# One map instead of two: the difference of two softmax maps formed before the transpose, in a two-block transformer on one core

## The reference, cut to what matters

```python
logits = jnp.einsum('bqhmd,bkhmd->bhmqk', qb, k).astype(jnp.float32) * scale + bias
logits = jnp.where(rel >= 0, logits, -jnp.inf)
p = jax.nn.softmax(logits, axis=-1)
w = p[:, :, 0] - lam * p[:, :, 1]
return jnp.einsum('bhqk,bkhe->bqhe', w.astype(v.dtype), v)
```

## Time and profile before

| | us |
|---|---|
| median of 3 runs | 4071.55 (4066.73 to 4072.94) |
| span of the profiled execution, first to last instruction | 4059.8 |
| PE busy | 3739.4 (92%) |
| DVE busy | 2398.3 (59%) |
| ACT busy | 1795.8 (44%) |
| POOL busy | 301.1 (7%) |
| PE's share of the chain that ended last | 83% |

### The profile page before, as it was taken

One profiled execution on the slowest core, in us unless ns is written; L12 is line 12 of the kernel. 1 busy time (PEld: TensorE's weight loads), 2 busy tenths in 40 slices (PEclk: granted clock), 3 DMA queues, 4 the chain that ended last, 5 costly groups with the idle time before them and its releaser, 6 DMA issues.

```text
span 4059.8 us, 52830 instructions
## 1 busy us (share of the span) xinstructions
PE 3739.4 (92%) x19920; PEld 2885.1 (71%) x19920; DVE 2398.3 (59%) x3434; ACT 1795.8 (44%) x2906; POOL 301.1 (7%) x385
## 2 busy tenths in 40 slices
PE   8998897998999587998999998899999999889998
PEld 7885575666787355555887776788777878657877
DVE  7865945887875876986774327566333332564332
ACT  3336644897333754886322326422233222453222
POOL 0110001110210001000220000111000000000001
PEclk9999587999999677999999999999999999999999
DMA  7551013997653014995774320277323223302222
GB/s 274 180 164 53 2 63 123 348 369 258 212 189 113 1 54 147 369 364 201 269 269 158 107 91 8 103 235 234 109 87 125 97 90 104 146 22 89 95 95 75
DMA packets 165090, 618.38 MB, mean 152 GB/s; under 512 B 18668, under 2 KB 20245, under 8 KB 163709
## 3 DMA queue, kind: packets, MB, share of 16 engines
q1 hardware_dynamic: 118384, 433.15, 30.3%
q0 software_dynamic: 42240, 154.16, 11.8%
q10 hardware_dynamic: 4238, 27.90, 1.8%
HBM read 595.94 MB, written 16.31 MB: 151 GB/s over the span
## 4 chain that ended last, share of the span: by engine, by line
PE 83%; DVE 8%; ACT 4%; issue 2%; DMA 2%; SPq 0%; ACTq 0%; DVEq 0%; POOL 0%; POOLq 0%; PEldq 0%
PE psum L2243 23%; PE psum L2256 12%; PE psum L830 12%; PE psum L2011 8%; PE psum L915 5%; PE psum L2030 4%; PE psum L982 4%; PE psum L759 3%; PE psum L1199 1%; PE psum L1209 1%; PE psum L767 1%; DVE spare L1305 1%; DMA ring<-wtile 1%; PE psum L1967 1%; PE psum L1483 1%
## 5 line engine op out<-in xcount | busy, mean ns | idle before, releaser
L783 ACT CAST small_r<-ring 128x1024 fp32r<-128x1024 f32 x264 | 276.1, 1048 | 1075.1 <-PE psum L830 335.5
L787 DVE TENSOR_TENSOR ring_r<-ring,small_r 128x1024 fp32r<-128x1024 f32 x264 | 322.7, 1225 | 686.7 <-ACT small_r L783 686.2
L783 ACT CAST PB_r<-ring 128x1024 fp32r<-128x1024 f32 x344 | 357.5, 1050 | 567.8 <-PE psum L2243 326.8
L787 DVE TENSOR_TENSOR ring_r<-ring,PB_r 128x1024 fp32r<-128x1024 f32 x344 | 414.2, 1222 | 270.6 <-ACT PB_r L783 269.2
L2243 PE MATMUL psum<-H_r,ring_r 128*128 128x512 f32 x1344 | 335.2, 391 | 0.0
L2243 PE MATMUL psum<-H_r,small_r 128*128 128x512 f32 x1344 | 327.7, 396 | 0.0
L2243 PE MATMUL psum<-H_r,PB_r 128*128 128x512 f32 x1344 | 318.3, 389 | 0.0
L2243 PEld LDWEIGHTS psum<-H_r,small_r 128*128 128x128 f32 x1344 | 253.0, 188 | 60.8
L2243 PEld LDWEIGHTS psum<-H_r,ring_r 128*128 128x128 f32 x1344 | 252.2, 188 | 55.2
L2243 PEld LDWEIGHTS psum<-H_r,PB_r 128*128 128x128 f32 x1344 | 252.3, 188 | 53.2
L830 PE MATMUL psum<-H_r,small_r 128*128 128x512 f32 (+1 forms) x1040 | 275.0, 368 | 0.1
(11 more groups left out here) (406 smaller groups left out, 6953.9 us busy)
## 6 DMA issues: line engine op xcount, KB each, us to landing
ring<-wtile SPq DMA_DIRECT2D x800, 512.0 KB, 4.9
spare<-wmod POOLq DMA_DIRECT2D x97, 512.0 KB, 4.9
H<-wmod POOLq DMA_DIRECT2D x48, 512.0 KB, 4.5
PB<-wmod POOLq DMA_DIRECT2D x48, 512.0 KB, 4.2
X<-wmod POOLq DMA_DIRECT2D x47, 512.0 KB, 4.9
h_rows<-PB POOLq DMA_DIRECT2D x10, 512.0 KB, 3.6
PB<-wmod SPq DMA_DIRECT2D x4, 1024.0 KB, 15.4
PB<-wshift SPq DMA_DIRECT2D x4, 1024.0 KB, 17.4
```

The source lines that it names most:

```text
L783: nc.scalar.copy(high(j), slot(g0 + j)).then_inc(high_ready.sem, 1)
L787: nc.vector.tensor_tensor(low(g0 + j), slot(g0 + j), high(j).bitcast(F32), ALU.subtract).then_inc(low_ready.sem, 1)
```

## The change

The stage gets a function of its own, `causal_pairs`, in place of `attention`.

- The scale of the scores moves into the copies of the projected queries (`form`).
- `BT2` grows to 512 columns a head; the DMA fills the last 256 and one copy on ACT spreads the constant value over the first 256.
- Bias, sign and minimum are one operation for each map (`tensor_tensor_reduce`), which replaces the scaled addition and the separate maximum.
- The difference of the maps, up to the factor 1/sum of map 0, is formed on DVE ahead of the transposes (`mixed`): reciprocal of the sums, ratio, and one operation of the unit's width. Then only one map is turned, copied and multiplied, and the output needs one operation (`taken_out`).
- PE's order is scores(u+2), turn(u), product(u-1); DVE's is biased(u+2), mixed(u), taken_out(u-2); ACT's is exponentials(u+1), keep_turned(u). There are three buffers of scores in place of two, and two PSUM banks for the turned map.

```diff
+            def ten(eng):
+                def scores(u):
+                    h, j = units[u]
+                    if u >= 2:
+                        eng.wait_ge(max_ready.sem, b_mx + u - 1)
+                    for m in range(2):
+                        r = slice(DH * m, DH * m + DH)
+                        mm = nc.tensor.matmul(scores_in(u, m), QK2(h)[r, j * P:(j + 1) * P], QK2(A_HEADS + h)[r, 0:width(u)], start=True, stop=True)
+                    mm.then_inc(scores_ready.sem, 1)
+                def turn(u):
+                    eng.wait_ge(probs_ready.sem, b_mi + u + 1)
+                    if u >= 2:
+                        eng.wait_ge(probsT_copied.sem, b_tc + u - 1)
+                    for t in range(width(u) // P):
+                        mm = nc.tensor.transpose(turned(u)[:, t * P:(t + 1) * P], kept(u, 0)[:, t * P:(t + 1) * P], ident)
+                    mm.then_inc(probsT_ready.sem, 1)
+                def product(u):
+                    eng.wait_ge(probsT_copied.sem, b_tc + u + 1)
+                    if u >= 2:
+                        eng.wait_ge(out_copied.sem, b_oc + u - 1)
+                    for t in range(j + 1):
+                        mm = nc.tensor.matmul(result(u), MIX_T[u % 2][:, t * P:(t + 1) * P], V2[:, t, h * P:(h + 1) * P], start=(t == 0), stop=(t == j))
+                    mm.then_inc(out_ready.sem, 1)
+                scores(0)
+                scores(1)
+                for u in range(n):
+                    scores(u + 2)
+                    turn(u)
+                    product(u - 1)
+                product(n - 1)
...
+            def sca(eng):
...
+                nc.scalar.copy(BT2[:, :, 0:NLAT - 2 * P], BT2[:, :, NLAT - 2 * P:NLAT - 2 * P + 1].broadcast_to([P, A_HEADS, NLAT - 2 * P])).then_inc(far_filled.sem, 1)
+                exponentials(0)
+                for u in range(n):
+                    exponentials(u + 1)
+                    keep_turned(u)
+                    if u >= 3:
+                        on_act(eng, u - 3)
...
+            def vec(eng):
+                def biased(u):
...
+                    if u >= 3:
+                        eng.wait_ge(probsT_ready.sem, b_tu + u - 2)
+                    eng.wait_ge(scores_ready.sem, b_sr + u + 1)
+                    for m in range(2):
+                        ins = nc.vector.tensor_tensor_reduce(kept(u, m), scores_in(u, m), BT2[:, h, NLAT - width(u):NLAT], -1.0, -NEG, ALU.add, ALU.min, accum_out=least(u)[:, m:m + 1])
+                    ins.then_inc(max_ready.sem, 1)
+                def mixed(u):
+                    eng.wait_ge(exp_ready.sem, b_ex + u + 1)
+                    V(eng, nc.vector.reciprocal(inverse(u), sums(u)))
+                    V(eng, nc.vector.scalar_tensor_tensor(share(u), sums(u)[:, 0:1], LAMBDA, inverse(u)[:, 1:2], ALU.mult, ALU.mult))
+                    nc.vector.scalar_tensor_tensor(kept(u, 0), kept(u, 1), share(u), kept(u, 0), ALU.mult, ALU.add).then_inc(probs_ready.sem, 1)
+                def taken_out(u):
+                    eng.wait_ge(out_ready.sem, b_or + u + 1)
+                    nc.vector.tensor_scalar(OTOK[:, j, h * P:(h + 1) * P], result(u), inverse(u)[:, 0:1], None, ALU.mult).then_inc(out_copied.sem, 1)
+                biased(0)
+                biased(1)
+                for u in range(n + 2):
+                    biased(u + 2)
+                    if u < n:
+                        mixed(u)
+                    if u >= 2:
+                        taken_out(u - 2)
+                    if u >= 4:
+                        on_dve(eng, u - 4, b_oc + u - 3)
...
-            freed = project("qkv", 0, 16, SLIM, lambda j, w: QK2(j), no_ctx(16), weights=weights, normed=normed, more=2)
+            freed = project("qkv", 0, 16, SLIM, lambda j, w: QK2(j), no_ctx(16), weights=weights, normed=normed, more=2,
+                            form=lambda j: (ACT.Copy, DH ** -0.5 if j < A_HEADS else 1.0))
...
-            attention(units, S3, ET3, rb[:, 0:128], [(0, 1), (2, 3)], True, (on_act, on_dve, last_on_act, last_on_dve))
+            causal_pairs(on_act, on_dve, last_on_act, last_on_dve)
...
-            eng.dma_start(BT2, bass.AP(tensor=rel_rows.tensor, offset=P - 1, ap=[[REL_W - 1, P], [P * REL_W, A_HEADS], [1, 2 * P]])).then_inc(rel_loaded.sem, 16)
+            eng.dma_start(BT2[:, :, NLAT - 2 * P:NLAT], bass.AP(tensor=rel_rows.tensor, offset=P - 1, ap=[[REL_W - 1, P], [P * REL_W, A_HEADS], [1, 2 * P]])).then_inc(rel_loaded.sem, 16)
```

More of the change, by code:

```diff
@@ L279, in build @@
         lam_ready = sig("lam_ready")
+        far_filled = sig("far_filled")
         forget_summed, forget_taken, forget_log, forget_ready = sig("forget_summed"), sig("forget_taken"), sig("forget_log"), sig("forget_ready")
@@ L2313, in build @@
         V2 = PB[:, 8192:8192 + 4096].rearrange("p (t n) -> p t n", t=4)
-        S3 = [PB[:, 16384 + b * 2 * NLAT:16384 + (b + 1) * 2 * NLAT] for b in range(2)]
-        ET3 = [PB[:, 18432 + b * 2 * NLAT:18432 + (b + 1) * 2 * NLAT] for b in range(2)]
-        BT2 = PB[:, 20480:20480 + 2048].rearrange("p (h n) -> p h n", h=A_HEADS)
+        BT2 = PB[:, 12288:12288 + A_HEADS * NLAT].rearrange("p (h n) -> p h n", h=A_HEADS)
+        S3 = [PB[:, 16384 + b * 2 * NLAT:16384 + (b + 1) * 2 * NLAT] for b in range(3)]
+        MIX_T = [PB[:, 19456 + b * NLAT:19456 + (b + 1) * NLAT] for b in range(2)]
         OTOK = H[:, 0:4096].rearrange("p (j n) -> p j n", j=4)
@@ L2325, in build, with causal_pairs, exponentials, keep_turned @@
         no_ctx = lambda n: [False] * n
+        def causal_pairs(on_act, on_dve, last_on_act, last_on_dve):
+            units = [(h, j) for h in range(A_HEADS) for j in range(4)]
+            n = len(units)
+            b_sr, b_mx, b_ex, b_mi, b_tu, b_tc, b_or, b_oc = (z.reserve(n) for z in (
+                scores_ready, max_ready, exp_ready, probs_ready, probsT_ready, probsT_copied, out_ready, out_copied))
+            b_far = far_filled.reserve(1)
+            width = lambda u: (units[u][1] + 1) * P
+            scores_in = lambda u, m: bank[2 * (u % 2) + m][:, 0:width(u)]
+            kept = lambda u, m: S3[u % 3][:, m * NLAT:m * NLAT + width(u)]
+            least = lambda u: rb[:, 2 * u:2 * u + 2]
+            sums = lambda u: rb[:, 2 * n + 2 * u:2 * n + 2 * u + 2]
+            inverse = lambda u: small[:, 2 * u:2 * u + 2]
+            share = lambda u: small[:, 2 * n + u:2 * n + u + 1]
+            turned = lambda u: bank[4 + u % 2][:, 0:width(u)]
+            result = lambda u: bank[6 + u % 2][:, 0:P]
+            def ten(eng):
+                def scores(u):
+                    if u >= n:
+                        return
+                    h, j = units[u]
[13 more added lines that the diff above has]
+                def product(u):
+                    if u < 0:
+                        return
+                    h, j = units[u]
+                    eng.wait_ge(probsT_copied.sem, b_tc + u + 1)
[12 more added lines that the diff above has]
+            def sca(eng):
+                def exponentials(u):
+                    if u >= n:
+                        return
+                    eng.wait_ge(max_ready.sem, b_mx + u + 1)
+                    for m in range(2):
+                        ins = nc.scalar.activation(kept(u, m), kept(u, m), ACT.Exp, bias=least(u)[:, m:m + 1], scale=-1.0, accum_out=sums(u)[:, m:m + 1])
+                    ins.then_inc(exp_ready.sem, 1)
+                def keep_turned(u):
+                    eng.wait_ge(probsT_ready.sem, b_tu + u + 1)
+                    if u >= 2:
+                        eng.wait_ge(out_ready.sem, b_or + u - 1)
+                    nc.scalar.copy(MIX_T[u % 2][:, 0:width(u)], turned(u)).then_inc(probsT_copied.sem, 1)
+                eng.wait_ge(rel_loaded.sem, 16)
+                nc.scalar.copy(BT2[:, :, 0:NLAT - 2 * P], BT2[:, :, NLAT - 2 * P:NLAT - 2 * P + 1].broadcast_to([P, A_HEADS, NLAT - 2 * P])).then_inc(far_filled.sem, 1)
[5 more added lines that the diff above has]
+                        on_act(eng, u - 3)
+                for u in range(n - 3, n):
+                    on_act(eng, u)
+                last_on_act(eng)
+            def vec(eng):
+                def biased(u):
+                    if u >= n:
+                        return
+                    h, j = units[u]
+                    if u == 0:
+                        eng.wait_ge(rel_loaded.sem, 16)
+                    if u == 2:
+                        eng.wait_ge(far_filled.sem, b_far + 1)
+                    if u >= 3:
+                        eng.wait_ge(probsT_ready.sem, b_tu + u - 2)
+                    eng.wait_ge(scores_ready.sem, b_sr + u + 1)
+                    for m in range(2):
+                        ins = nc.vector.tensor_tensor_reduce(kept(u, m), scores_in(u, m), BT2[:, h, NLAT - width(u):NLAT], -1.0, -NEG, ALU.add, ALU.min, accum_out=least(u)[:, m:m + 1])
[6 more added lines that the diff above has]
+                def taken_out(u):
+                    h, j = units[u]
```

(14 more changed lines are left out.)

## The result

The changed kernel takes 4120.31 us (4117.65 to 4131.1, four runs), the kernel before, on the same chip, 4069.14 (4059.6 to 4072.94, four runs). The ratio is 1.0133, 95% interval 1.0114 to 1.0153: slower by about 51 us. The forecast was 4124, with a range from 4084 to 4146.

The account below looks back on a forecast made before the run. No engine is full, so the order of waits bounds the stage. At 19.6 us a head it lasts 160.6 us, 52.5 more than 108.1; added to the median 4071.55 that gives 4124 us, range 4084 to 4146.

Parts of the forecast that it names:

- The ring: In the stage of `differential`'s attention, PE and DVE take turns, each waiting for the other: 15.7 us a head at full clock.
- the clock stays: Rival: PE's clock in the stage stays at 2.4 GHz, 15.7 us a head, +22.6, 4094 us; chance 0.20.
- VectorE's share: DVE's part of a head in the stage: 3.6 us for the fused pairs plus 3.8 for mixing, 7.4.
- The second pass: Rival: the fused operation on DVE passes twice over the columns, +2.7 us a head, 21 us, 4145; chance 0.10.
- The overlap of 0.07 us between neighbours: Neighbouring DVE operations start 0.07 us closer than their durations; used in costing the fused pairs at 3.6 us a head.
- The clock: PE's rests in the stage lower its clock: three quarters of the time at 1.2 GHz, 19.6 us a head.
- The sum: Stage: 4.8 ahead + 151.6 - 4.5 + 8.7 behind = 160.6 us, 52.5 more than 108.1; kernel 4124 us.
- The engines overlap: Rival: scores(u+3) not held behind turn(u), so DVE sets the pace at 9.8 us a head, 4053 us; chance 0.07.
- ACT stayed hidden: ACT's work in the stage, under 9.9 us a head, lies beside the 15.7 us and adds nothing.

Follow-up runs that it names:

- E1: Changed kernel with mixed(u) moved ahead of biased(u+2) in VectorE's order, nothing else: 4052.09 us, ratio 0.9965 to the kernel before.
- E2: Changed kernel with scores(u+3) put ahead of turn(u) on TensorE, VectorE's order kept: 4056.13 us, ratio 0.9967 to the kernel before.
- E3: Changed kernel with two unread matmuls of 384 columns ahead of each turn(u), one bank for the turned map: 4087.23 us, ratio 1.0049 to the kernel before.

## Why the prediction was right, step by step

**The ring.** Right, and the cause of the loss: E1 and E2 cut it at two places, and each turns 1.3% slower into 0.3% faster. Its price at full clock was put at 15.7 us a head; E3 measures 15.34. E3 also bears out the case "the clock stays": 22.6 us over before were worked out, 22.2 measured (4087.23 against 4065.02).

**VectorE's share.** Right to a few hundredths: 689 ns for 512 columns against 683 assumed, the reading of the minimum beside the next operation, 751 for the mix against 744. The second pass did not come. The overlap of 0.07 us between neighbours doesn't follow from the row that was named for it (one piece of 0.75 us, 0.75 to the next start), but the new operations show it: those of 128 columns take 0.29 us and start 0.22 apart (2444.72 and 2444.94). Both sources of the mix lie in SBUF; at half rate its slope would be near 2.1 ns a column, an estimate from twice the 1.05 of the prediction, and from 128 to 512 columns it is (751 - 352) / 384 = 1.04. The Trainium skill, Vector Engine (DVE) Microarchitecture Reference, section 7, halves the rate of such an operation; this trace does not bear it out.

**The clock.** Right in direction and in size: three quarters of the time at 1.2 GHz were assumed, and the stage's grant of 0.62 is that. In its middle it was lower: from the transposes of 2460.51 to those of 2580.74 the grant was 0.60, four fifths low, and six heads took 20.04 us each, against 19.6 in the sum. The loss has two parts: about 22 us for the order at the high clock (E3 against before), and some 30 more because PE's rests lower the clock. The 22 are net of what the change saves. Against E1, the same arithmetic without the ring, the order costs 35 us (4087.23 against 4052.09) and the clock 33 more. The Trainium skill, TensorE: Matmul & The Clock Gate, section "A second HAM failure mode: psum-queue depth-cycling", tells of brief rests of PE that let the clock swing; the swing in this trace agrees, and E3 ends it by filling the rests.

**The sum.** The 11.75 us between the median and the profiled span were read as what lies around the span. They are mostly the spread between executions: the profiled execution of the changed kernel took 4117.71 us with a span of 4115.9, 1.8 around it. The forecast adds the stage's change to the median, so nothing hung on it. The stage was put at 160.6 us and took 163.0. The start up to the first mix was 3.4 in place of 4.8, since the scores of 384 columns there still ran at the high clock. From the first to the last mix it was 148.1 in place of 147.1. Here two errors met. The sum takes off 3.2 us for three units without scores, but by the order in the code only two sets are missing there, those of 128 and 256 columns: 1.7 us by the prediction's own half-clock rows, so about -3.0 in place of -4.5. The longer heads of the middle came on top, and the first heads and the last ones saved more than that. Behind the start of the last mix it was 11.6 in place of 8.7: the mix itself (1.2) was left out of that term, and in place of an output and a clamp ACT had four squares, each with the reading of its sum, and eight scalings to do there (2598.46 and 2599.63), 3.5 us. The terms are off by -1.4, +1.0 and +2.9, and partly cancel. That 4120.31 stands within 4 us of 4124 is closer than the terms are, and closer than the measurement can tell: some luck is in it.

**The other rivals.** "The engines overlap" was right about what an uncut ring would leave: 9.8 us a head and 4053 were worked out; E1 has 10.7 in the mean and 4052, E2 9.9 and 4056. It was rightly given little chance for this code, since the order stands in it. ACT stayed hidden up to the last two units, where the chain passes once through a copy and two exponentials (2593.64 to 2595.43), and the copy of 2048 columns (1.9 us) lay beside the first scores.

## What to carry to other kernels

Before moving an operation from one engine to another, write down the orders of both and look for a cycle: each engine's next step held behind the step that waits for the other. Then the price of an instruction is paid whole however idle its engine is, and busy shares say nothing; the chain that changes engine in every unit, and two large waits in opposite directions (here 82.0 and 62.7 us), are how it looks in a profile. The cure is to move one call ahead of the other: here that gained 68 us, where the change as it stood had lost 51. When rests appear on TensorE, read the granted clock of the stretch too: here the slower clock more than doubled the loss.

## What the runs showed of the hardware

- The clock rose and fell about once a head and stood at 2.4 GHz for a quarter of the time, in a stage where PE was busy for 94.2 of 165 us with rests of up to 2.4 us. With the rests filled (107.6 of 127 us busy) it was at 1.00, and the kernel 33 us shorter for 49.6 us more work.
- The fused operation with a minimum appears as a custom instruction at the rate of a plain two-tensor operation (689 ns for 512 columns), and its reading of the minimum (83 ns) runs beside the next one: in the changed kernel's timeline the reading and the second operation of 384 columns both start at 2446.84.
